# A hybrid-mixer and MoE layer kernel: the S5 rotation angles as one VectorE addition per pair instead of 16 GpSimd operations, and a second buffer for one held block

## The chip, the cores and the metric

One core of a Trainium2 chip runs the whole kernel in one launch. The time is device microseconds (us) of that core. Engines are called PE (TensorE), DVE (VectorE), ACT (ScalarE), POOL (GpSimd) and SP (SyncE, which issues most of the DMAs). Each runs its own instruction stream in order, and they meet only at semaphores.

## The reference, cut to what matters

The input is 512 tokens of width 2048. An input projection feeds four mixers of width 512 (S5, RG-LRU, RWKV7, SSD), an output projection follows, then a mixture of experts with 64 experts and two choices per token, and a final norm. The change touches the S5 mixer and the storing of the input projection:

```
dt = exp(log_dt);  mag = exp(lambda_re * dt)
abar = mag * (cos(lambda_im * dt) + i sin(lambda_im * dt))
state[t] = abar * state[t-1] + Bbar u[t]          # complex, 32 groups of 64 states
y = Re(C state) + d * u;  y = gelu(y);  y = y * sigmoid(y @ w_glu + b_glu);  rms_norm
```

The kernel takes the rotation out of the recurrence: it multiplies the input by exp(-i t theta), runs two real scans with the factor mag, and multiplies back by exp(i t theta). So it needs, for each of 128 states (two groups, a "pair"), the cosine and sine of t theta at all 512 times t. There are 16 pairs. The angle, in turns, is the sum of a fine part (t mod 32: 32 values) and a coarse part (t div 32: 16 values), both kept in `turns[:, p, 0:48]`.

## The kernel before, in words

**Projection.** PE first computes six ordinary column tiles (n = 0 to 5; loop at L2621 and L2627), four of which are the S5 input U5. Tile n may start once ACT has copied out tile n-2 (`proj_out`, L1118). All other columns are done as 16 "fast slabs" f of 256 columns by Strassen's method in Winograd's form: 7 products b = 0 to 6 of 8 K-slices each (L2660), where each K-slice is recorded as two matmuls of 256 columns. Product number g = 7f + b may start when ACT has taken product g-2 out of PSUM (`take_product`, L1132). Products 0, 2 and 4 go into the held blocks `held[0..2]`; POOL later adds each to a block that ACT stored (`add_held`, L912). ACT may fill held block k again once POOL has added the one of the slab before (semaphore `added`).

**Weight sums.** Some products need sums of weight blocks. POOL issues three accumulating DMAs per slab: `sum1` (L890), `sum2` (L895) and `sum3` (L899), for slab f+1 during slab f, at b = 3, 5 and 6. A fourth sum, needed by product (f, 3), is one 128x1024 addition: on DVE for f = 0 to 5 (`weight_sum`, L1662), on POOL from then on (L905). SP loads the weight blocks; the block for product g is asked for when product g-7 is done.

**S5 pairs.** PE places S5 work at fixed K-slices of the projection, counted by u, with u = 76 + 8g + k from the first fast slab on. One step comes every 25 K-slices: at step p (even) PE computes the inputs of pairs p and p+1 (`s5_in_mm`, L2461; it waits until DVE has read those of pair p-1), and at steps 5, 9, 13, 17 the outputs of four finished pairs (`s5_out_mm`, L2473). DVE runs `s5_pair(p)` in order (L1537, L1677, L1683, L1684, L1696, L1698), with the weight sums of slabs 0 to 5 at fixed half pairs: before pair 3, in the middle of pairs 5 and 7, before pairs 10 and 12, in the middle of pair 14.

**Angles and tables.** POOL's `wrap(p)` makes the 128x512 angles of a pair by 16 operations of 128x32 (L860), each adding one coarse value to the 32 fine ones. It writes into the second half of the pair's table buffer; there are three such buffers, so wrap(p) waits until pair p-3 is done with its tables. wrap(0 to 2) run ahead of the first sum1, wrap(3) and wrap(4) between sum1(0), sum2(0) and sum3(0), and the others behind given products:

```
            wrap_at = {(S5_EVERY * p - 112) // 8: p for p in range(5, NPAIR)}
```

ACT's `table(p, r)` (L1150 to L1154) waits for the angles and makes the cosine (r = 0) and sine (r = 1) by three activations each. Tables 0, 1 and 2 stand behind the copy of tile 1, tables 3 and 4 behind those of tiles 3 and 4, the others behind given products.

**After the S5 pairs** DVE makes the RG-LRU convolution, the norms, the SSD and RWKV7 steps; PE goes on through the slabs, the RWKV7 chunks, the output projection and the experts, whose weights stream from HBM.

Of the kernel before, what the change touches and what calls it, by code (L numbers as in the profile page):

```python
# [7 lines left out]
P = 128  # L8
# [96 lines left out]
def build(nc, I, out):  # L105
    with ExitStack() as ctx:
# [133 lines left out]
        held = [wo_more[:, 0, 0:256], wo_more[:, 0, 256:512], wo_more[:, 1, 0:256]]  # L240
# [244 lines left out]
        wrap_ok, WRAP = tr_used_act, 4  # L485
# [33 lines left out]
        def slabs_done(eng, n):  # L519
            eng.wait_ge(took, TOOK + PB_ * n)  # L520
            eng.wait_ge(added, ADDED + 3 * n)

# [275 lines left out]
        def _(pool):  # L798
# [56 lines left out]
            def wrap(p):  # L855
                turn = s5tab[p % 3][:, 1, :]
                if p >= 3:
                    pool.wait_ge(tab_used, p - 2)
                for k in range(COARSE):
                    last = nc.gpsimd.tensor_scalar(turn[:, FINE * k:FINE * k + FINE], turns[:, p, 0:FINE],  # L860
                                                   turns[:, p, FINE + k:FINE + k + 1], None, ALU.add)
                last.then_inc(wrap_ok, 1)

# [11 lines left out]
            for p in range(3):  # L875
                wrap(p)
# [30 lines left out]
            def add_held(f, k):  # L907

                n, t, reads = ((0, 1, 4), (1, 1, 5), (0, 0, 6))[k]
                pool.wait_ge(took, TOOK + PB_ * f + reads)  # L910
                o = block_out(f, n, t)
                nc.gpsimd.tensor_tensor(o, o, held[(1, 2, 0)[k]], ALU.add).then_inc(added, 1)  # L912

            sum1(0)
            wrap(3)
            sum2(0)
            wrap(4)
            sum3(0)
            wrap_at = {(S5_EVERY * p - 112) // 8: p for p in range(5, NPAIR)}
            for f in range(NF):  # L920
                for b in range(PB_):
                    if b == 0 and f >= S5_SUMS:
                        sum4(f)
                    if b == 3 and f < NF - 1:
                        sum1(f + 1)
                    if b == 4:
                        add_held(f, 0)
                    if b == 5:
                        add_held(f, 1)
                        if f == Z_END:  # L930
                            pool.wait_ge(dtv_ok, 2)
                            k, i = at[("xt", NTT - 1)]
                            pool.wait_ge(full[k], i + 1)
                            triangle(0)
                            triangle(1)
                        if f < NF - 1:
                            sum2(f + 1)
                    if b == 6:
                        add_held(f, 2)
                        if f < NF - 1:  # L940
                            sum3(f + 1)
                        if f in (Z_END + 1, Z_END + 2):
                            triangle(f - Z_END + 1)
                    if PB_ * f + b in wrap_at:
                        wrap(wrap_at[PB_ * f + b])

# [124 lines left out]
        def _(act):  # L1071
# [48 lines left out]
            def take_product(f, b):  # L1120

                act.wait_ge(prod_ok, PROD + PB_ * f + b + 1)
                if b in (0, 2, 4):
                    if f:

                        act.wait_ge(added, ADDED + 3 * f - (0, 2, 1)[b // 2])
                    to = held[b // 2]
# [18 lines left out]
            def table(p, r):  # L1146
                x, out = s5tab[p % 3][:, 1, :], s5tab[p % 3][:, r, :]
                if r == 0:
                    act.wait_ge(wrap_ok, WRAP + p + 1)
# [97 lines left out]
            for n in range(NT):  # L1247
                if n:
                    proj_out(n)
                if n == 1:  # L1250
                    s5_setup()
                    for p in range(3):
                        table(p, 0)
                        table(p, 1)
                if n in (3, 4):
# [228 lines left out]
        def _(dve):  # L1484
# [161 lines left out]
            v.do(nc.vector.tensor_reduce(out=stacked[:], in_=ident[:].rearrange("p (g t) -> p t g", g=2), op=ADD, axis=AX))  # L1646
            op(T4, B22, T1, ADD)
# [16 lines left out]
            def s5_pair(p):  # L1664
# [32 lines left out]
                v.settle()  # L1697
                v.tell(nc.vector.tensor_tensor(xi, k[0], k[2], ADD), st_ok, p + 1)  # L1698
# [1412 lines left out]
```

## Time and profile before

| | us |
|---|---|
| median of 3 runs | 2458.86 (2458.52 to 2463.66) |
| the profiled execution's own time | 2459.19 |
| its span, first to last instruction | 2457.4 |
| busy: PE / DVE / ACT / POOL | 2265.4 / 816.2 / 456.7 / 549.0 |
| mean granted TensorE clock | 0.971 |
| time outside the span | 1.8 |

The last line is the difference of the second and the third. Busy times of different engines lie beside each other and don't add up; a wait counts only where the chain that ended last runs through it. In the rows below a line number names the instruction's line of the kernel before, and "[x <- R]" is idle time of that engine just before the instruction, with what ended it.

### The profile page before, as it was taken

Reading aid. Unit: us, or ns where it says so; the run is one execution under the profiler, and the core shown is the slowest. Engines: PE = TensorE matmul, PEld = TensorE weight load, DVE = VectorE, ACT = ScalarE, POOL = GpSimd, SP = SyncE. Lnnn points to the kernel's source line nnn. Section 1 sums busy time; section 2 is a strip of 40 time slices with the busy share of each in tenths; the row PEclk is TensorE's granted clock in tenths of the full one; section 3 lists DMA queues with packets and bytes.
Section 4 is the critical chain, followed back from the end, with each engine's and each line's share of the span. In section 5 each row is a group of like instructions: output and inputs, shape, how many; then the busy total and the mean of one; then the engine's idle time right before and its main releaser. Section 6 shows DMA issues by size and latency. Waiting matters only on the chain.

```text
span 2457.4 us, 34178 instructions
## 1 busy us (share of the span) xinstructions
PE 2265.4 (92%) x13339; PEld 1302.2 (53%) x13339; DVE 816.2 (33%) x1331; ACT 456.7 (19%) x796; POOL 549.0 (22%) x845
## 2 busy tenths in 40 slices
PE   8999999999999999999998888888888898888888
PEld 4476868885566646544444444444444444444443
DVE  6689775256444332311111111111111111111114
ACT  3433262114222222000000000000000000000002
POOL 5799423331322110111111111111111111111110
PEclk9999999999999999999999999999999999999999
DMA  5477869873302445899999999999999999999998
GB/s 179 95 162 153 182 137 191 184 160 115 104 20 78 148 175 204 344 423 426 427 424 426 427 425 426 427 427 425 427 427 425 427 427 425 426 427 426 424 427 368
DMA packets 236939, 759.80 MB, mean 309 GB/s; under 512 B 35928, under 2 KB 173468, under 8 KB 193084
## 3 DMA queue, kind: packets, MB, share of 16 engines
q1 hardware_dynamic: 173464, 710.29, 72.3%
q0 software_dynamic: 54016, 42.00, 9.6%
q10 hardware_dynamic: 9380, 6.40, 0.8%
q8 instruction: 56, 0.92, 0.2%
q14 instruction: 23, 0.19, 0.0%
HBM read 753.23 MB, written 47.19 MB: 326 GB/s over the span
## 4 chain that ended last, share of the span: by engine, by line
PE 48%; DMA 41%; POOL 6%; DVE 3%; issue 1%; ACT 1%; SPq 0%; DVEq 0%; POOLq 0%; ACTq 0%
DMA big<-in_moe_w 39%; PE ps L3005 12%; PE ps L2660 12%; PE ps L2727 6%; POOL big L860 5%; PE ps L3036 4%; PE ps L2882 2%; PE ps L2802 1%; DMA big<-in_norm_final 1%; PE ps L3021 1%; PE ps L2627 1%; PE ps L2787 1%; PE ps L2989 1%; PE ps L2675 1%; PE ps L2495 1%
## 5 line engine op out<-in xcount | busy, mean ns | idle before, releaser
L3005 PE MATMUL ps<-big 128*64 128x384 f32 x4096 | 695.6, 494 | 96.4 <-DMA big<-in_moe_w 85.7
L3005 PEld LDWEIGHTS ps<-big 128*64 128x64 f32 x4096 | 305.3, 138 | 492.9 <-issue 343.6
L3036 PE MATMUL ps<-big 128*64 128x512 f32 x1536 | 386.7, 657 | 57.0 <-DVE big L2352 57.0
L2660 PE MATMUL ps<-big 128*128 128x256 f32 x1792 | 396.8, 382 | 8.1 <-ACT wo_more L1132 5.5
L2660 PEld LDWEIGHTS ps<-big 128*128 128x128 f32 x1792 | 340.3, 191 | 67.5 <-issue 14.5
L3036 PEld LDWEIGHTS ps<-big 128*64 128x64 f32 x1536 | 124.8, 150 | 272.0 <-issue 240.9
L2348 DVE TENSOR_SCALAR big<-ps,scal 128x384 f32<-128x384 f32 x64 | 39.6, 618 | 688.9 <-PE ps L3005 688.9
L2357 DVE SCALAR_TENSOR_TENSOR big<-ps,scal,big 128x512 f32<-128x512 f32 x128 | 90.2, 747 | 399.3 <-PE ps L3036 399.3
L1033 POOL COPY scal<-slots 128x3 f32 (+1 forms) x64 | 12.0, 188 | 909.7 <-DVE big L2357 891.4
L1454 ACT ACTIVATE big<-ps,scal 128x384 f32<-128x384 f32 x64 | 37.2, 581 | 799.4 <-PE ps L3005 770.8
L860 POOL TENSOR_SCALAR big<-big 128x32 f32<-128x32 f32 x256 | 160.1, 1449 | 0.1
L2727 PE MATMUL ps<-big 128*128 128x512 f32 x320 | 154.4, 611 | 1.0 <-ACT big L1217 0.7
L3021 PE MATMUL ps<-stacked,big 128*128 128x64 f32 x768 | 141.2, 334 | 0.0
L3021 PEld LDWEIGHTS ps<-stacked,big 128*128 128x128 f32 x768 | 138.8, 261 | 0.8 <-issue 0.8
L1459 ACT ACTIVATE big<-ps 128x192 f32<-128x192 f32 x64 | 21.2, 332 | 516.4 <-PE ps L3021 516.4
L1537 DVE TENSOR_TENSOR big<-big 128x512 f32<-128x512 f32 (+5 forms) x132 | 103.9, 807 | 20.8 <-ACT big L1173 10.1
L2727 PEld LDWEIGHTS ps<-big 128*128 128x128 f32 x320 | 55.9, 189 | 56.6 <-issue 50.8
L2272 DVE TENSOR_TENSOR big<-ps,gffn 128x512 f32<-128x512 f32 x128 | 82.5, 686 | 0.6
L2989 PEld LDWEIGHTS ps<-ident,big 128*128 128x128 f32 x512 | 62.0, 194 | 37.7 <-issue 37.7
L1029 POOL DMA_INDIRECT big<-x_rows,gix x62 | 65.2, 1052 | 54.4 <-POOL gix L1025 54.4
L912 POOL TENSOR_TENSOR big<-big,wo_more 128x256 f32<-128x256 f32 x48 | 56.5, 1239 | 84.3 <-ACT big L1132 57.6
L1043 POOL DMA_INDIRECT y_rows<-big,six x62 | 62.8, 1014 | 55.1 <-POOL six L1040 51.5
(444 smaller groups left out, 2003.4 us busy)
## 6 DMA issues: line engine op xcount, KB each, us to landing
big<-in_moe_w SPq DMA_DIRECT2D x187, 3072.0 KB, 38.7
big<-in_w_in SPq DMA_DIRECT2D x96, 512.0 KB, 4.4
big<-in_w_in POOLq DMA_DIRECT2D x32, 512.0 KB, 7.5
big<-in_moe_w SPq DMA_DIRECT2D x6, 1536.0 KB, 8.8
big<-big POOLq DMA_DIRECT2D x16, 512.0 KB, 5.3
big<-in_w_out SPq DMA_DIRECT2D x8, 1024.0 KB, 5.3
big<-y_rows SPq DMA_DIRECT2D x8, 1024.0 KB, 28.1
big<-in_x SPq DMA_DIRECT2D x4, 1024.0 KB, 8.4
```

Source lines behind the costliest of these rows:

```text
L860: last = nc.gpsimd.tensor_scalar(turn[:, FINE * k:FINE * k + FINE], turns[:, p, 0:FINE], turns[:, p, FINE + k:FINE + k + 1], None, ALU.add)
L1029: nc.gpsimd.indirect_dma_start(xg[k], None, x2g, bass.IndirectOffsetOnAxis(ap=of, axis=0), bounds_check=T * GR - 1, oob_is_err=False).then ...
L1043: nc.gpsimd.indirect_dma_start(ydg, bass.IndirectOffsetOnAxis(ap=six[k][:, 0:1], axis=0), yb[k], None, bounds_check=2 * T * GR - 1, oob_is ...
L1537: v.do(nc.vector.tensor_tensor(out, a, b, o))
L2272: nc.vector.tensor_tensor(xT[k][:, cs, :].rearrange("p c (g t) -> p c g t", g=GR), ps[h][:, 0:NJ * P // 2].rearrange("p (c g t) -> p c g t ...
L2357: nc.vector.scalar_tensor_tensor(out=yb[k][:, cs], in0=ps[5 + q][:], scalar=scal[k][:, 0:1], in1=yb[k][:, cs], op0=MUL, op1=ADD).then_inc( ...
L2660: last = nc.tensor.matmul(o, w[:, k, :], side[:, k, :], start=(k == 0 and b in (0, 1, 5)), stop=(k == 7), skip_group_check=True)
L2727: last = nc.tensor.matmul(ps[b][:], ready[c][:, P * i:P * i + P], wo_mix[c], start=(c == 0), stop=(c == PO - 1), skip_group_check=True)
L2989: last = nc.tensor.transpose(ps[h][:, P * j:P * j + P], xg[k].rearrange("t (p c) -> t c p", c=NJ)[:, c], ident[:])
L3005: last = nc.tensor.matmul(ps[2 + w][B * g:B * g + B, 0:FF], xT[k][:, j, B * g:B * g + B], W13[k][w][:, NJ * g + j, :], start=(j == 0), sto ...
L3021: last = nc.tensor.matmul(o, uv[k][:, w, :].rearrange("p (t c) -> p c t", c=FC)[:, m], stacked[:], start=True, stop=True)
L3036: last = nc.tensor.matmul(ps[5 + q][B * g:B * g + B, :], hid[k][:, m, :], W2[k][:, m, 512 * n:512 * n + 512], start=(m == 0), stop=(m == F ...
```

## The change

POOL's `wrap` and all its calls go. DVE makes the angles of a pair by one addition of 128x512 with both operands broadcast: those of pairs 0, 1 and 2 in its set-up, behind the reduction that makes `stacked` and ahead of the two 128x2048 operations of T4; those of pair p+3 inside `s5_pair(p)`, between the last product with the table and the last addition of the pair. ACT makes tables 0 and 1 behind the copy of tile 1 and table n behind the copy of tile n for n = 2, 3, 4. `held` gets a fourth block, which stands in for block 0 in slabs 1, 3, 5 and 7; in slabs below 8, ACT's wait before it fills block 0 asks for the additions of one slab less.

```
-        held = [wo_more[:, 0, 0:256], wo_more[:, 0, 256:512], wo_more[:, 1, 0:256]]
+        held = [wo_more[:, 0, 0:256], wo_more[:, 0, 256:512], wo_more[:, 1, 0:256], wo_more[:, 1, 256:512]]
...
+        HELD2 = 8
+        def held_of(f, k):
+            return held[3 if k == 0 and f % 2 and f < HELD2 else k]
...
-            def wrap(p):
-                turn = s5tab[p % 3][:, 1, :]
-                if p >= 3:
-                    pool.wait_ge(tab_used, p - 2)
-                for k in range(COARSE):
-                    last = nc.gpsimd.tensor_scalar(turn[:, FINE * k:FINE * k + FINE], turns[:, p, 0:FINE],
-                                                   turns[:, p, FINE + k:FINE + k + 1], None, ALU.add)
-                last.then_inc(wrap_ok, 1)
...
-            for p in range(3):
-                wrap(p)
...
-                nc.gpsimd.tensor_tensor(o, o, held[(1, 2, 0)[k]], ALU.add).then_inc(added, 1)
+                nc.gpsimd.tensor_tensor(o, o, held_of(f, (1, 2, 0)[k]), ALU.add).then_inc(added, 1)
             sum1(0)
-            wrap(3)
             sum2(0)
-            wrap(4)
             sum3(0)
-            wrap_at = {(S5_EVERY * p - 112) // 8: p for p in range(5, NPAIR)}
...
-                    if PB_ * f + b in wrap_at:
-                        wrap(wrap_at[PB_ * f + b])
...
-                        act.wait_ge(added, ADDED + 3 * f - (0, 2, 1)[b // 2])
-                    to = held[b // 2]
+                        act.wait_ge(added, ADDED + 3 * f - (0, 2, 1)[b // 2] - (3 if b == 0 and f < HELD2 else 0))
+                    to = held_of(f, b // 2)
...
-                    act.wait_ge(wrap_ok, WRAP + p + 1)
+                    act.wait_ge(angle_ok, ANGLE + p + 1)
...
-                    for p in range(3):
-                        table(p, 0)
-                        table(p, 1)
-                if n in (3, 4):
+                    table(0, 0)
+                    table(0, 1)
+                if 1 <= n <= 4:
                     table(n, 0)
                     table(n, 1)
...
+            def angles(p):
+                v.tell(nc.vector.tensor_tensor(s5tab[p % 3][:, 1, :].rearrange("p (a b) -> p a b", a=COARSE),
+                                               turns[:, p, FINE:].unsqueeze(2).to_broadcast([P, COARSE, FINE]),
+                                               turns[:, p, 0:FINE].unsqueeze(1).to_broadcast([P, COARSE, FINE]), ADD), angle_ok, ANGLE + p + 1)
+            for p in range(3):
+                angles(p)
             op(T4, B22, T1, ADD)
...
                 v.tell(nc.vector.tensor_tensor(k[2], cosT, k[3], MUL), tab_used, p + 1)
                 v.settle()
+                if p + 3 < NPAIR:
+                    angles(p + 3)
+                    v.settle()
                 v.tell(nc.vector.tensor_tensor(xi, k[0], k[2], ADD), st_ok, p + 1)
```

## Rows read from the trace of the kernel before

**Rows 1.** The chain that ended last, by engine and by line, whole run.

```profile
PE 48%; DMA 41%; POOL 6%; DVE 3%; issue 1%; ACT 1%; SPq 0%; DVEq 0%; POOLq 0%; ACTq 0%
DMA big<-in_moe_w 39%; PE ps L3005 12%; PE ps L2660 12%; PE ps L2727 6%; POOL big L860 5%; PE ps L3036 4%; PE ps L2882 2%; PE ps L2802 1%; DMA big<-in_norm_final 1%; PE ps L3021 1%; PE ps L2627 1%; PE ps L2787 1%; PE ps L2989 1%; PE ps L2675 1%; PE ps L2495 1%
```

**Rows 2.** Windows: stretch, length, busy us (count) per engine, granted clock, DMA share, GB/s.

```profile
84.00:88.00 4.00, 3.01 (x8) 1.14 (x10) 3.91 (x5) 1.31 (x3) 0.00 (x0) 0.60 1.10 298
236.00:240.00 4.00, 3.27 (x8) 2.64 (x9) 3.93 (x6) 3.60 (x7) 4.00 (x6) 0.50 0.49 58
300.00:500.00 200.00, 200.00 (x917) 163.64 (x916) 106.39 (x152) 70.27 (x107) 68.11 (x53) 1.00 0.84 175
1600.00:2400.00 800.00, 700.68 (x3788) 342.72 (x3787) 127.34 (x211) 68.31 (x106) 88.41 (x173) 0.96 1.01 426
```

**Rows 3.** The chain that ended last, 0 to 800 us: start, us, what.

```profile
55.45 24.39 POOL big L860 x48
```

**Rows 4.** Timeline of PE, 50 to 300 us: start, us, work, [idle before <- releaser].

```profile
84.99 8.69 PE L2621 MATMUL ps<-big 128*64 128x512 f32 x32 [2.53 <-ACT big L1118]
...
146.68 1.53 PE L2660 MATMUL ps<-big 128*128 128x256 f32 x6 [1.75 <-DMA big<-big]
...
176.06 9.73 PE L2660 MATMUL ps<-big 128*128 128x256 f32 x44 [0.74 <-DMA big<-big]
...
212.84 11.06 PE L2660 MATMUL ps<-big 128*128 128x256 f32 x50 [1.30 <-ACT wo_more L1132]
...
236.74 7.09 PE L2660 MATMUL ps<-big 128*128 128x256 f32 x20 [4.25 <-ACT wo_more L1132]
...
258.52 32.99 PE L2660 MATMUL ps<-big 128*128 128x256 f32 x150
291.44 1.92 PE L2473 MATMUL ps<-big 128*32 128x512 f32 x16
```

**Rows 5.** Timeline of ACT, same columns, 50 to 330 us.

```profile
79.87 0.72 ACT L1150 ACTIVATE big<-big,zero 128x512 f32<-128x512 f32 x1 [4.75 <-POOL big L860]
...
236.30 0.38 ACT L1132 ACTIVATE wo_more<-ps 128x256 f32<-128x256 f32 x1 [11.39 <-POOL big L912]
```

**Rows 6.** Timeline of POOL, same columns, 50 to 320 us.

```profile
235.21 0.99 POOL L912 TENSOR_TENSOR big<-big,wo_more 128x256 f32<-128x256 f32 x1
```

**Rows 7.** POOL by line, 55 to 262 us: work, count, busy us, mean ns, idle before.

```profile
L860 POOL TENSOR_SCALAR big<-big 128x32 f32<-128x32 f32 x256 | 160.1, 1449 | 0.1
```

**Rows 8.** Timeline of DVE, 38 to 320 us: steps of S5 pairs 0, 1 and 3.

```profile
77.58 2.75 DVE L1537 TENSOR_TENSOR big<-big 128x512 f32<-128x512 f32 x4
80.25 0.68 DVE L1696 TENSOR_TENSOR big<-big 128x512 f32<-128x512 f32 x1
80.96 0.69 DVE L1698 TENSOR_TENSOR big<-big 128x512 f32<-128x512 f32 x1
...
88.01 2.75 DVE L1537 TENSOR_TENSOR big<-big 128x512 f32<-128x512 f32 x4
...
126.33 1.75 DVE L1696 TENSOR_TENSOR big<-big 128x512 f32<-128x512 f32 x1
```

**Rows 9.** Timeline of DVE: weight sum 0 and every later idle up to weight sum 5.

```profile
116.26 1.23 DVE L1662 TENSOR_TENSOR big<-big 128x1024 f32<-128x1024 f32 x1 [5.88 <-DMA big<-in_w_in]
...
146.73 1.22 DVE L1662 TENSOR_TENSOR big<-big 128x1024 f32<-128x1024 f32 x1 [0.66 <-DMA big<-big]
...
176.11 1.26 DVE L1662 TENSOR_TENSOR big<-big 128x1024 f32<-128x1024 f32 x1 [6.19 <-DMA big<-big]
...
233.43 1.25 DVE L1662 TENSOR_TENSOR big<-big 128x1024 f32<-128x1024 f32 x1 [3.98 <-DMA big<-big]
...
258.63 1.89 DVE L1537 TENSOR_TENSOR big<-ps,big 128x512 f32<-128x512 f32 x3 [1.73 <-PE ps L2461]
...
268.01 1.23 DVE L1662 TENSOR_TENSOR big<-big 128x1024 f32<-128x1024 f32 x1 [2.16 <-PE ps L2660]
```

**Rows 10.** DVE by line and shape, 39 to 45.7 us: additions and products with broadcast operands.

```profile
L1537 DVE TENSOR_TENSOR big<-tk,s5v 128x768 f32<-128x768 f32 x2 | 1.8, 954 | 0.0
```

More of the change, by code:

```diff
@@ L482, in build @@
         WEIGHT_IN = [16 * len(PA), 16 * (len(PB) + 2), 16 * 8, 0, 16 * ((len(slabs) + 1) // 2), 16 * (len(slabs) // 2), NTT]
-        wrap_ok, WRAP = tr_used_act, 4
+        angle_ok, ANGLE = tr_used_act, 4
         s1_in, s2_in, s3_in = xg_in[0], xg_in[1], y_out[0]
```

## The prediction

> **What bounds the kernel now.** I began with the page's chain of work that ended last: PE holds 48% of it and DMA 41%, almost all of that the expert weights, and one POOL line, L860, holds 5% [rows 1]. L860 is what the change removes, so 5% of 2457.4 us (123 us) looks like the prize. It is not, for a chain names one engine for each stretch and doesn't say how close the next one runs behind. The windows answer that: in the expert stage the DMA share is 1.01 at 426 GB/s, and from 300 to 500 us PE is busy for 200.00 of 200 us at full clock [rows 2]. Neither stretch can gain; both can only start earlier. The chain's pieces with L860 begin at 55 us [rows 3] and end near 236 us, and there the question is how much PE, which runs in a fixed order from the first tile to the experts, really stood still.
>
> So I went to PE's timeline. From 50 to 292 us it has five idle stretches: 2.53 + 1.75 + 0.74 + 1.30 + 4.25 = 10.57 us [rows 4]. Behind the first and the last the granted clock lay low, 0.60 from 84 to 88 us and 0.50 from 236 to 240 us, the lower level (1.2 GHz) for part or all of these windows [rows 2]. The first costs (1 - 0.60) x 4 = 1.6 us. For the last I count: 20 matmuls took 7.09 us, at the pace of the later row (32.99 us for 150, or 0.220 us each) they take 4.40, so 2.7 us more [rows 4]. Together PE lost 10.57 + 1.6 + 2.7 = **14.9 us**.
>
> Who held PE each time? At 82.5 us it waited for ACT's copy of tile 2, which stood behind table 2, and ACT waited 4.75 us for L860 [rows 4, 5]: POOL needed 24.39 us for three pairs [rows 3]. At 146.7 and 176.1 us it waited for a DMA within SBUF (sum2), which POOL issues in order behind its wraps [rows 4]. At 212.8 us it was ACT again. At 236.7 us PE waited for ACT, which had waited 11.39 us for POOL's addition of a held block, itself only done at 235.21 + 0.99 us [rows 4 to 6]. Here 16 operations, a sum2 and its DMA wait stood ahead of the addition. POOL had no time to spare: L860 took 160.1 us of the 207 from 55 to 262 us, and before it POOL was idle for 0.1 us [rows 7].
>
> **The change part by part.**
>
> *Wraps off POOL.* The 256 operations keep POOL busy for 160.1 us, 0.63 us each (the mean of 1.449 us counts records that overlap) [rows 7]. Off the path they are worth nothing; on it they are worth PE's four stalls from 146 us on, and the first by way of ACT. What POOL has left are three DMA issues and three additions per slab. Is a transfer late next? From 300 to 500 us no wraps are there, the slabs follow each other as densely, and PE has no idle time [rows 2]. So I take nothing for the DMAs. If that cover is gone, a late sum costs what it does now, 0.7 to 1.8 us each [rows 4].
>
> *Order of the tables on ACT.* Table 2 moves behind the copy of tile 2. ACT makes tables 0 and 1 by about 75 us, as now (its wait for table 2 began at 79.87 - 4.75 = 75.1) [rows 5], copies tile 2, and tile 4 starts on PE at 82.5 us. The 2.53 us go, and with them I expect the low clock to go; if that comes from tile 4 itself, 1.6 us stay. Tables 3 and 4 need angles that DVE makes at the end of pairs 0 and 1, about 81 and 93 us, in time for copies at 83 and 90 us within 3 us that nobody waits for.
>
> *Second held block.* ACT's wait of 11.39 us has two answers in this change, the wraps' removal and this buffer. Either would do, so it gets no gain of its own. If POOL were still late, it would be worth up to the 4.25 + 2.7 us [rows 4].
>
> *Angles on DVE.* The trace has no 128x512 sum of two broadcast SBUF operands. The nearest row has the same forms at 768 elements: 0.954 us [rows 10]. A 128x512 of two plain SBUF operands takes 0.68 us, and starts of two that wait for each other lie 80.96 - 80.25 = 0.71 us apart [rows 8]. Bounds: 0.954 x 512/768 = 0.64 us from below, and from above 1.75 us, which the instruction of 0.68 us took when it met POOL's addition [rows 8]. I take **0.71 us**, from the rows of the same size. The three of the set-up, 2.1 us, lie in DVE's idle 10 us before pair 0 and delay only T4, needed at product 6. Ten of the other 13 (pairs 3 to 12) are in the stretch that matters.
>
> *What is late next: DVE.* Its tightest meeting with PE is weight sum 5, in pair 14. DVE's real work from weight sum 0 (start 116.26) to the end of sum 5 (268.01 + 1.23 = 269.24) is 152.98 us less the idle 0.66 + 6.19 + 3.98 + 1.73 + 2.16 = 14.72, so 138.26 us [rows 9]. Sum 0 waits for a weight block asked for at the end of tile 5, so it moves with PE: 116.26 - 2.53 - 1.6 = 112.1. With ten angles DVE is through sum 5 at 112.1 + 138.3 + 7.1 = 257.5 if it never idles. The DMA waits in this list are all of the kind that earlier sums shorten, so it hardly will. POOL's additions slow DVE where they meet (1.75 against 0.68) [rows 8], and a tenth of its old time (14.72 of 152.98) was idle, in which some of them fell; I add 0.8 us: **258.3 us**.
>
> PE needs it at product (5, 3), which is 60 matmuls into the row that starts at 258.52: 258.52 + 60 x 0.220 = 271.7 [rows 4]. Without the 14.9 us that is **256.8 us**. PE thus waits 1.5 us for DVE. The two earlier meetings (inputs of pairs 12 and 14) come out within half a microsecond. Pair 15 ends some 16 us behind sum 5 (half of pair 14 and pair 15 at 10.5 us each, and collisions), 274.5, and PE wants it at 291.44 - 14.9 + 1.5 = 278.0, so nothing more is lost.
>
> *Sum.* 14.9 - 1.5 = 13.4 us. From 292 us on every start hangs on PE's order or on buffers that it frees, so the expert stream starts as much earlier and the gain passes whole. 2459.19 - 13.4 = 2445.8 for the profiled execution. That execution lies 0.3 us over the median of the runs, so I say **2445.5 us**.
>
> *A rule to weigh.* DVE's four products of a pair took 2.75 us both while POOL ran 48 wraps (at 77.58) and while POOL had nothing to do (at 88.01) [rows 8], so by the rows taking wraps away gives DVE nothing. The Trainium skill, page "SBUF — State Buffer", section "SBUF: two separate sides", says otherwise: a DVE operation with two SBUF inputs and a GpSimd operation that reads SBUF take turns on one port pair, and whoever comes second is blocked for the whole instruction. By that, DVE would get time back here and the 1.5 us of waiting would go: 2444. On POOL's side the trace may bear it out (0.63 us per wrap over all, but 24.39/48 = 0.51 in the first three pairs, where DVE was idle for 10 us) [rows 3, 7], and DVE's 1.75 us beside an addition of POOL as well [rows 8]. By the same rule each new addition can hold up a POOL addition for 0.7 us, which POOL now has room for.
>
> **Rivals.**
>
> *A. PE alone is the bound.* DVE keeps up, because collisions are fewer or POOL's two-input additions fall into PSUM reads. Gain 14.9 us: 2444.0, and if the restarts behind the five stalls cost a little more than I counted, 2442.5. For it: the margin is only 1.5 us, and the page's rule. Against: DVE would have no idle left at all.
>
> *B. DVE becomes the real bound.* Each addition costs more like 1.2 us, or the collisions double as POOL and DVE now meet in every slab. Ten times 0.4 us more: gain 9 us, 2450. For it: the row of 1.75 us. Against: most steps of a pair show 0.68 to 0.71.
>
> *C. The stalls move to the weight DMAs.* PE now asks for blocks some 8% faster, sum2 waits for its block and PE for sum2. Four waits of 1.5 us and one low clock of 2.7 us take 9 us back: gain 4 to 5 us, 2455. Against: the dense stretch from 300 us [rows 2].
>
> *D. Slower.* DVE is in order, and the addition stands ahead of the state that PE waits for. If it costs c instead of 0.71 us, the gain 13.4 falls by 10(c - 0.71); it is gone at c = 2.05 us and the kernel is 5 us slower at c = 2.55 us, 2464. That takes a collision in every pair, each longer than the longest shown; this mechanism decides nothing below 2 us.
>
> *E. It doesn't do what it says:* the first stall stays, since tile 4 waits for something else too. Gain 13.4 - 4.1, 2449.5; counted with B.
>
> **How the numbers follow.** Forecast (2445.5, its own range 2443.5 to 2447.5): 50%. A 20%, B and E 19%, C 8%, D 3%. 0.2% is 4.9 us, about what a measurement of this kernel tells from no change. Faster by more: the forecast, A, B and half of C, 0.93. Within: half of C and a third of D, 0.05. Slower: 0.02. The range runs from 2441.5 (A with its margin) to 2450.5 (B), and leaves out C and D, 11%, and some at the low end.
>
> **What would show it.** PE without idle at 82 us and at 232 us, and no low clock behind them. POOL's busy time lower by 150 us or more and DVE's higher by 16 x 0.6 to 0.7 us, about 11. sum2(1) and sum2(2) issued some 10 us earlier against PE's product. If the forecast is right, DVE has next to no idle from pair 3 to pair 15, PE has one or two waits for DVE (L1662 or L1677) of 2 us together between 190 and 260 us, and output step 17 starts near 278 us (277 under A, 282 under B). An angle addition over 1 us would make the step on DVE wrong; PE waiting for DMA within the slabs would make C right; an expert stream that doesn't start 13 us earlier would make the passing on wrong.

## The result and the profile after

The changed kernel took **2439.62 us** (median of 4 runs, 2438.55 to 2445.99), the kernel before beside it 2461.26 (4 runs); ratio 0.9916, 95% interval 0.9892 to 0.9940. The forecast was 2445.5 us, in a range of 2441.5 to 2450.5. The kernel is faster, as said, but by the ratio the gain is 0.0084 x 2461.26 = 20.7 us, half as large again as the 13.4 of the sum, and the time lies 1.9 us under the range. The profiled execution took 2440.12 us with a span of 2438.4; before it was 2459.19 and 2457.4, so 19.0 us of span.

The page's chain of work that ended last, by engine and by line, beside [rows 1]:

```profile
PE 52%; DMA 44%; DVE 2%; issue 1%; ACT 0%; POOL 0%; ACTq 0%; DVEq 0%; SPq 0%; POOLq 0%
DMA big<-in_moe_w 43%; PE ps L2657 16%; PE ps L3002 10%; PE ps L2724 6%; PE ps L2624 3%; PE ps L3033 3%; PE ps L2879 2%; PE ps L2799 1%; DMA big<-in_norm_final 1%; PE ps L2784 1%; PE ps L3018 1%; PE ps L2458 1%; PE ps L2672 1%; PE ps L2492 1%; PE ps L2900 1%
```

POOL's 6% are 0% and no POOL line is left. PE and DMA have taken the share over, which is the point of the first section of the prediction: the 5% of L860 were not the prize.

Three of the windows of [rows 2] (stretch, length, busy us of PE, PEld, DVE, ACT and POOL, granted clock, DMA share, GB/s):

```profile
84.00:88.00 4.00, 4.00 (x22) 1.41 (x20) 3.93 (x6) 3.10 (x5) 0.00 (x0) 1.00 1.11 301
236.00:240.00 4.00, 4.00 (x21) 3.51 (x20) 3.93 (x5) 2.82 (x5) 1.82 (x3) 1.00 0.73 178
...
1600.00:2400.00 800.00, 699.82 (x3802) 343.09 (x3798) 127.72 (x211) 68.19 (x105) 85.85 (x168) 0.97 1.01 426
```

The clock stands at 1.00 where it was 0.60 and 0.50. The stretch of the experts is what it was, DMA share 1.01 at 426 GB/s. It only begins earlier: PE's first expert product starts at 976.02 us where it started at 994.93.

PE's timeline from 50 to 300 us (start, us, work); beside [rows 4]:

```profile
82.25 7.09 PE L2618 MATMUL ps<-big 128*64 128x512 f32 x32
...
143.72 21.85 PE L2657 MATMUL ps<-big 128*128 128x256 f32 x100
165.51 1.99 PE L2458 MATMUL ps<-big 32*128 32x512 f32 x8
...
242.62 32.64 PE L2657 MATMUL ps<-big 128*128 128x256 f32 x150
275.19 1.92 PE L2470 MATMUL ps<-big 128*32 128x512 f32 x16
```

No row of this view shows idle time any more. Tile 4 takes 7.09 us instead of 8.69, and output step 17 starts at 275.19 instead of 291.44: **16.25 us** at the end of the S5 stage. Product (5, 3), which the prediction took for the tightest meeting with DVE, starts 60 matmuls into the row of 242.62, 242.62 + 60 x 32.64/150 = 255.7 us. The row at 165.51 is the input step of pairs 8 and 9.

DVE's timeline, beside [rows 8, 9]; L1635 is the addition of the angles, L1656 the weight sum, and L1671 the instruction with which DVE is through reading a pair's inputs:

```profile
56.11 1.88 DVE L1635 TENSOR_TENSOR big<-big 128x512 f32<-128x512 f32 x3
...
80.77 0.69 DVE L1635 TENSOR_TENSOR big<-big 128x512 f32<-128x512 f32 x1
...
111.90 1.23 DVE L1656 TENSOR_TENSOR big<-big 128x1024 f32<-128x1024 f32 x1 [5.18 <-DMA big<-in_w_in]
...
163.04 0.68 DVE L1671 TENSOR_TENSOR big<-ps,big 128x512 f32<-128x512 f32 x1
...
180.28 3.16 DVE L1524 TENSOR_TENSOR big<-big 128x512 f32<-128x512 f32 x4
...
251.87 1.22 DVE L1656 TENSOR_TENSOR big<-big 128x1024 f32<-128x1024 f32 x1
```

The three additions of the set-up start at 56.11 and lie in idle time. Within a pair one takes 0.69 us, and its neighbours start 0.72 us apart, as priced. From the start of sum 0 (111.90) to the end of sum 5 (251.87 + 1.22 = 253.09) DVE works 141.2 us without idle time; the sum in the prediction had 146.2 and an end at 258.3. The row at 180.28 is a hold-up, a DVE operation that takes longer than usual beside a POOL addition: 3.16 us where 2.75 is usual. The longest single one in this stretch is 0.54 us. DVE is 2.6 us early for product (5, 3) (253.1 against 255.7), but less for the inputs: it has read those of pair 7 at 163.04 + 0.68 = 163.7 and PE comes for them at 165.5, 1.8 us later, and at the step of pairs 12 and 13 2.0 us later (212.9 against 214.95).

POOL's timeline, beside [rows 6, 7]:

```profile
122.09 1.09 POOL L907 TENSOR_TENSOR big<-big,wo_more 128x256 f32<-128x256 f32 x1
125.22 0.73 POOL L907 TENSOR_TENSOR big<-big,wo_more 128x256 f32<-128x256 f32 x1 [2.03 <-ACT wo_more L1120]
...
173.10 1.53 POOL L885 DMA_DIRECT2D big<-in_w_in  x1 [13.81 <-DMA big<-in_w_in]
```

POOL waits for DMAs and for ACT, and each held-block addition runs alone, soon after ACT's store. Busy time of POOL fell from 549.0 to 400.6 us, that of DVE rose from 816.2 to 820.9 where 16 additions alone are 11 us, so everything else on DVE takes some 6 us less. The prediction's signs were 150 us or more and about 11 us; POOL's fall of 148.4 is just under the one, DVE's rise of 4.7 far under the other.

### The profile page after: what moved, and what is told of

Read it like the earlier page. It is cut to its first block, busy times and chain, and to the rows that moved or that the text cites. A ratio compares the mean times of both kernels' runs of the same rounds, so it can differ in the third digit from the quotient of the medians.

```text
span 2438.4 us, 33939 instructions
## 1 busy us (share of the span) xinstructions
PE 2248.5 (92%) x13339; PEld 1294.0 (53%) x13339; DVE 820.9 (34%) x1347; ACT 456.3 (19%) x796; POOL 400.6 (16%) x589
## 4 chain that ended last, share of the span: by engine, by line
PE 52%; DMA 44%; DVE 2%; issue 1%; ACT 0%; POOL 0%; ACTq 0%; DVEq 0%; SPq 0%; POOLq 0%
DMA big<-in_moe_w 43%; PE ps L2657 16%; PE ps L3002 10%; PE ps L2724 6%; PE ps L2624 3%; PE ps L3033 3%; PE ps L2879 2%; PE ps L2799 1%; DMA big<-in_norm_final 1%; PE ps L2784 1%; PE ps L3018 1%; PE ps L2458 1%; PE ps L2672 1%; PE ps L2492 1%; PE ps L2900 1%
## 5 line engine op out<-in xcount | busy, mean ns | idle before, releaser
L3018 PE MATMUL ps<-stacked,big 128*128 128x64 f32 x768 | 141.2, 334 | 0.0
L2986 PE MATMUL ps<-ident,big 128*128 128x128 f32 x512 | 74.1, 288 | 1.6 <-DMA big<-x_rows,idxg 1.6
L1444 ACT ACTIVATE big<-big,scal 128x1024 f32<-128x1024 f32 x64 | 72.8, 1137 | 0.0
```

The lines of the kernel that those rows point to most:

```text
L1444: nc.scalar.activation(yb[k], xg[k], ACT.Copy, scale=scal[k][:, 2:3]).then_inc(pre_ok[k], 1)
L2986: last = nc.tensor.transpose(ps[h][:, P * j:P * j + P], xg[k].rearrange("t (p c) -> t c p", c=NJ)[:, c], ident[:])
L3018: last = nc.tensor.matmul(o, uv[k][:, w, :].rearrange("p (t c) -> p c t", c=FC)[:, m], stacked[:], start=True, stop=True)
```

## The experiments

"Step 17" is the start of PE's last S5 output. It was 291.44 us in the trace before and 275.19 in the one after. The line numbers of each row are those of that run's own kernel.

**Which part of the change does it?** Four kernels, each with one part undone or one done alone.

e1, the changed kernel with the old order of tables:

```
+                    for p in range(3):
+                        table(p, 0)
+                        table(p, 1)
+                if n in (3, 4):
...
-                if 1 <= n <= 4:
```

> The changed kernel, but ACT makes tables 0, 1 and 2 behind the copy of tile 1, as before. Theory 1 (the angles' early arrival is all that counts): DVE has the angles of pair 2 by 58 us, ACT is through table 2 at about 79.5 us and copies tile 2 at 80.1, before PE wants it at 82.3 us. PE has no idle time at tile 4, output step 17 starts at 275.2 us as in the changed kernel, total within 1 us of it. Theory 2 (the new order carries the first stall, as the prediction had it): PE stops at 82 us, the clock falls behind it, step 17 starts 3 to 4 us later, 278.5 to 279.

Step 17 at 275.20 us, no idle time on PE; 2443.43 us (4 runs, 2439.98 to 2446.05), ratio 0.9920 (0.9898 to 0.9941). ACT's timeline (L1142 ends table 2, L1107 copies tiles 2 and 3):

```profile
78.51 0.72 ACT L1142 ACTIVATE big<-big,minus_halfpi 128x512 f32<-128x512 f32 x1
79.26 0.60 ACT L1107 ACTIVATE big<-ps 128x512 f32<-128x512 f32 x1
```

With angles from DVE table 2 ends at 79.23 and the copy is made at 79.26, three microseconds before PE needs it at 82.3. Theory 1 holds for the stage: once DVE makes the angles, the new order is worth nothing there.

e2, the changed kernel with one held block 0 (`HELD2 = 0`, and ACT's wait as before):

> The changed kernel with the held block 0 single again. Theory 1 (either answer would do): with the wraps gone POOL adds the held block within 1 to 2 us of ACT's store, ACT never waits for it, PE has no idle time, step 17 at 275.2 us, total within 1 us of the changed kernel. Theory 2 (the buffer carries part of the gain): ACT waits for POOL at some product 0 of slabs 1 to 7 and PE stops, step 17 later than 276 us.

Step 17 at 275.22 us, no idle time on PE, no wait of ACT for POOL; 2444.40 us (4 runs, 2440.28 to 2446.23), ratio 0.9926 (0.9903 to 0.9949). Theory 1 again: the second buffer does nothing once POOL is on time. Both theories also said a total within 1 us of the changed kernel; the two medians lie 3.8 and 4.8 us over its first one (2439.62), but 0.4 and 1.3 us over its second one (2443.06, e10 below). What differs lies behind step 17. The kernel without both parts at once was not run.

e3, the kernel before with the second held block alone:

```
-                to = held[b // 2]
+                to = held_of(f, b // 2)
```

> The kernel before with the second held block alone; wraps stay on POOL. Theory 1 (the stall at 232 us comes from the held block): ACT's wait of 11.4 us goes, and of PE's 4.25 us idle and 2.7 us of low clock about 5.5 us go, since sum2 of slab 4 lands only about 233.4 us and holds PE for under 1 us: step 17 at 285 to 286.5 us. Theory 2 (POOL is late by itself, whoever waits for it first): PE stops at product 2 or 3 of slab 4 or at a table instead, and the gain is under 2 us, step 17 at 289.5 us or later.

2459.19 us (10 runs), ratio 0.9993 (0.9981 to 1.0005), step 17 at 294.12: nothing gained (the kernel before had step 17 at 291.44 to 294.30, see e7 and e12). Three of PE's rows with idle time, and POOL's wrap 4 (L866), its sum2 (L901) and the wrap behind it:

```profile
84.13 7.09 PE L2627 MATMUL ps<-big 128*64 128x512 f32 x32 [1.76 <-ACT big L1124]
...
114.03 9.29 PE L2666 MATMUL ps<-big 128*128 128x256 f32 x34 [3.36 <-ACT big L1124]
...
239.53 7.25 PE L2666 MATMUL ps<-big 128*128 128x256 f32 x20 [4.16 <-DMA big<-big]
```

```profile
97.24 11.86 POOL L866 TENSOR_SCALAR big<-big 128x32 f32<-128x32 f32 x16
...
231.86 0.90 POOL L901 DMA_DIRECT2D big<-big  x1 [5.60 <-DMA big<-in_w_in]
232.49 5.49 POOL L866 TENSOR_SCALAR big<-big 128x32 f32<-128x32 f32 x16
```

ACT's 11.4 us wait went, and PE stopped just as long at 239.5 for sum2. POOL had issued that one late because it first had to see sum1 land, and sum1 stood behind two wraps (issued at 221.44, against 201.47 in the changed kernel). Theory 2: POOL is late, whoever waits first. A new stall stands at 114.03: wrap 4 took 11.86 us where it had taken 8.33, so table 4 and with it the copy of tile 5 came late. Here the first stall was shorter and tile 4 took 7.09 us, so PE ran 2.5 us ahead of the trace before, and this too was given back at 114.03.

e6, the kernel before with the angles of pairs 0 to 2 on DVE and the new order of tables:

```
-            for p in range(3):
-                wrap(p)
```

> The kernel before with the angles of pairs 0, 1 and 2 on DVE and the new order of the tables; wraps 3 to 15 stay on POOL, one held block. Theory 1 (stalls add up): the first stall and its low clock go (4.1 to 4.3 us), the later ones stay as they are, step 17 at 287.2 us. Theory 2 (POOL sets the pace from 115 to 236 us): PE is 4.3 us earlier at 105 us and waits longer later; at step 17 under 2 us are left, 289.5 us or later.

2461.29 us (10 runs), ratio 0.9993 (0.9981 to 1.0006), step 17 at 294.64. Two of PE's rows with idle time:

```profile
114.05 10.60 PE L2664 MATMUL ps<-big 128*128 128x256 f32 x34 [5.08 <-ACT big L1116]
...
239.85 6.14 PE L2664 MATMUL ps<-big 128*128 128x256 f32 x20 [4.01 <-ACT wo_more L1130]
```

The first stall is gone and 5.08 us stand at 114 us in its place: wrap 4 took 11.49 us here, for PE and with it DVE's pair 2 came earlier (95.09 us instead of 99.25) and fell onto the wrap. Theory 2, and more than it said: with this part alone the 4 us are given back within 32 us. So the stalls don't add up. POOL sets the pace from about 90 to 236 us, and of the kernels run only those that relieve POOL over that whole stretch gain. Moving wraps 3 to 15 alone was not tried.

**Why was DVE not late?**

e4, each addition of pairs 3 to 15 made twice:

```
+                    op(s5tab[p % 3][:, 1, :]..., turns[:, p + 3, FINE:]..., turns[:, p + 3, 0:FINE]..., ADD)
+                    v.settle()
                     angles(p + 3)
```

> The changed kernel with the addition of the angles of pairs 3 to 15 made twice in a row, same place. In the changed kernel weight sum 5 ends at 253.1 us and PE starts product (5, 3) at 255.7, so DVE has 2.6 us of room. Theory 1 (DVE was not the bound, but only just): ten more additions of 0.72 us put sum 5 at 260.3, PE waits for DVE by 4.6 us in all, step 17 starts at 279.5 to 280.2 us. Theory 2 (DVE has far more room than this, its order gives way): step 17 stays within 1 us of 275.2. Theory 3 (more two-input operations on DVE also meet POOL more, as the prediction's 0.8 us supposed): sum 5 later than 262 us, step 17 later than 281.5.

2446.78 us (4 runs), ratio 0.9945 (0.9930 to 0.9960). PE's rows with idle time:

```profile
166.44 1.99 PE L2462 MATMUL ps<-big 32*128 32x512 f32 x8 [0.80 <-DVE big L1671]
...
203.24 14.48 PE L2661 MATMUL ps<-big 128*128 128x256 f32 x66 [1.53 <-DVE big L1656]
218.75 1.99 PE L2462 MATMUL ps<-big 32*128 32x512 f32 x8 [1.02 <-DVE big L1671]
...
260.52 20.09 PE L2661 MATMUL ps<-big 128*128 128x256 f32 x92 [1.32 <-DVE big L1656]
```

PE waits for DVE four times, 4.67 us in all: for the inputs of pairs 8 and 12 and for weight sums 3 and 5. The prediction had named sum 5 and the inputs of pair 12. Sum 5 ends at 260.37, and step 17 comes at 280.54, 5.35 us late. Theory 1's mechanism, a shade above its band. DVE's room is real and small: ten times 0.72 us use it up and cost PE the rest. The first of the four waits comes at the meeting with 1.8 us of room.

e5, small POOL operations in POOL's idle time:

```
+                        if f < 6:
+                            for k in range(COARSE):
+                                g.do(nc.gpsimd.tensor_scalar(spare[:, FINE * k:FINE * k + FINE], spare_in[:], spare_in[:, k:k + 1], None, ALU.add))
+                            g.settle()
```

> The changed kernel, and POOL also runs 16 additions of 128x32 like a wrap (values that nobody reads, in buffers of their own) behind sum3 of slabs 1 to 6, where it is idle for some 13 us while DVE works on the pairs. DVE's work from the start of sum 0 to the end of sum 5 is 141.2 us without them. Theory A (small POOL operations don't slow DVE; what made DVE faster in the changed kernel is that POOL's 128x256 additions no longer come in bunches): it stays at 141 to 142, and 16 of them take POOL 11 to 12.5 us each time. Theory B (each takes the port from DVE): 5 x 16 of them cost DVE 4 us or more, 145 us and up, and PE waits for it. Under A step 17 stays at 275.2 to 276 us, under B it comes at 277 or later.

2444.12 us (4 runs), step 17 at 275.36. DVE's sums 0 and 5, and two of POOL's groups of 16:

```profile
111.54 1.22 DVE L1662 TENSOR_TENSOR big<-big 128x1024 f32<-128x1024 f32 x1 [4.64 <-DMA big<-in_w_in]
...
251.91 1.23 DVE L1662 TENSOR_TENSOR big<-big 128x1024 f32<-128x1024 f32 x1
```

```profile
213.46 12.93 POOL L938 TENSOR_SCALAR big<-spare_in 128x32 f32<-128x32 f32 x16
...
242.68 11.19 POOL L938 TENSOR_SCALAR big<-spare_in 128x32 f32<-128x32 f32 x16
```

From 111.54 to 251.91 + 1.23 are 141.6 us, against 141.2 without 80 extra operations (141.2 to 141.3 in all six traces of such kernels). Theory A: they don't slow DVE by more than 0.4 us in all. DVE slows them: 11.2 to 12.9 us for 16, where the three first wraps of the kernel before, with DVE idle for 10 of 24 us, took 8.1 each [rows 3].

e9, the same 18 held-block additions, but in slabs 0 to 5 in a row:

```
-                    if b == 4:
-                        add_held(f, 0)
...
                     if b == 6:
+                        if f < 6:
+                            add_held(f, 0)
+                            add_held(f, 1)
                         add_held(f, 2)
```

> The changed kernel, but in slabs 0 to 5 POOL does the three held-block additions back to back behind the last product of the slab instead of each behind its own. Nothing else is added, the same 18 additions. In the changed kernel DVE needs 141.2 us from the start of sum 0 to the end of sum 5, and its longest single hold-up beside an addition of POOL is 0.54 us; in the kernel before single hold-ups reached 1.77 us where two additions stood in a row. Theory 1 (bunches cost DVE more than the same additions apart): 143 to 146 us, hold-ups of over 1 us, and if sum 5 ends after 255.7 us PE waits for it. Theory 2 (each addition costs the same wherever it stands): 140.5 to 142 us, no hold-up over 0.6 us. The output step 17 of PE at 275.2 us under theory 2, up to 277 under theory 1.

Step 17 at 276.65; one run, 2441.14 us. Two of POOL's bunches, then DVE's operations beside them, and sum 5:

```profile
128.42 4.33 POOL L907 TENSOR_TENSOR big<-big,wo_more 128x256 f32<-128x256 f32 x3
...
208.86 1.73 POOL L907 TENSOR_TENSOR big<-big,wo_more 128x256 f32<-128x256 f32 x2
```

```profile
131.13 3.62 DVE L1528 TENSOR_TENSOR big<-big 128x512 f32<-128x512 f32 x4
...
206.62 4.52 DVE L1528 TENSOR_TENSOR big<-big 128x512 f32<-128x512 f32 x4
...
254.89 1.22 DVE L1660 TENSOR_TENSOR big<-big 128x1024 f32<-128x1024 f32 x1
```

DVE's work from sum 0 (112.13) to the end of sum 5 (256.11) is 144.0 us, 2.8 more than with the additions apart, and PE waits 1.29 us for it at the input step of pair 12. Four operations of 2.75 us take 3.62 beside the first bunch and 4.52 beside the other, there with a single hold-up of 1.77 us. That is theory 1. It bears out bunches as a cause, and 2.8 us of the difference.

The rest can be read off the traces. For every instruction of DVE between sum 0 and sum 5 I took what it needed beyond the usual time of its kind in the trace after, and added these up. POOL makes 15 held-block additions in this stretch in each of the four traces.

| trace | hold-ups, us in all | of these beside a POOL addition | longest |
|---|---|---|---|
| before | 8.9 | 8.4 | 1.77 |
| after | 4.5 | 4.5 | 0.54 |
| e9, bunched | 7.3 | 7.3 | 1.77 |
| e5, with 80 small operations | 5.0 | 4.6 | 0.55 |

The longest one before, beside three additions of POOL in 4.4 us (at 193.73 and 195.71); two of these DVE operations take 1.29 us elsewhere:

```profile
194.52 3.06 DVE L1537 TENSOR_TENSOR big<-big 128x512 f32<-128x512 f32 x2
```

So the same 15 additions cost DVE 8.4 us before and 4.5 after. Beside wraps alone it loses 0.6 us, in more than a hundred instructions.

**How firm are the times themselves?**

e7 and e12, the kernel before again:

> The kernel before once more, for how much one execution differs from another. Theory 1 (the S5 stage of the kernel before is a chain by way of POOL whose wraps take 5.5 to 12.4 us each, depending on what DVE does beside them): step 17 is not at 291.44 to the tenth but somewhere from 290 to 295 us. Theory 2 (only the clock at the routing stage varies, 30.5 or 34.6 to 36.6 us from the first triangle product to the first down product): step 17 at 291.4 within 0.3 us. Both can hold for the routing stage.

> The kernel before a third time. Its step 17 stood at 291.44 us in the trace that the prediction used and at 293.85 in the second. Theory 1 (the S5 stage of the kernel before differs from one execution to the next, since it hangs on how POOL's wraps fall against DVE's operations): again another time, between 290 and 295 us, and PE's stalls from 140 to 275 us again of other lengths. Theory 2 (two fixed patterns): 291.4 or 293.9 within 0.2 us with the same stalls.

2460.89 and 2458.73 us, step 17 at 293.85 and 294.30. PE's rows with idle time behind 120 us, e7 and then e12:

```profile
148.63 1.60 PE L2661 MATMUL ps<-big 128*128 128x256 f32 x6 [3.66 <-DMA big<-big]
...
239.12 6.05 PE L2661 MATMUL ps<-big 128*128 128x256 f32 x20 [3.94 <-ACT wo_more L1133]
...
270.37 23.55 PE L2661 MATMUL ps<-big 128*128 128x256 f32 x108 [1.18 <-DMA big<-big]
```

```profile
148.68 1.90 PE L2662 MATMUL ps<-big 128*128 128x256 f32 x6 [3.84 <-DMA big<-big]
...
239.02 5.97 PE L2662 MATMUL ps<-big 128*128 128x256 f32 x20 [3.56 <-ACT wo_more L1134]
...
270.82 23.55 PE L2662 MATMUL ps<-big 128*128 128x256 f32 x108 [1.81 <-DMA big<-big]
```

The stall of [rows 4] at 146.7 us lasts twice as long here, those at 176.1 and 212.8 us are missing, a new one stands at 270. With 291.44 this makes three times out of one program, and two of them share a pattern: theory 1 for the spread, with something of theory 2's patterns in it. In all six traces of kernels with the angles on DVE, POOL's additions where they belong and one addition per pair (after, e1, e2, e8, e10, e11) step 17 lies between 275.19 and 275.22.

At the routing stage the kernel chooses each token's experts. It runs from the first product with a triangular matrix ("triangle product") to the first expert's second product ("down product"), and fillers are matmuls whose results nobody reads, which keep PE busy in between.

e10, the changed kernel again, and e8 and e11, the changed kernel with more fillers:

```
-            keep_busy(24)
+            keep_busy(32)
...
-            keep_busy(8)
+            keep_busy(14)
...
-            keep_busy(4)
+            keep_busy(10)
```

> The changed kernel with more filler matmuls at the routing stage: 32, 14 and 10 in place of 24, 8 and 4, so that PE's idle times there (2.0, 1.6 and 1.6 us) are mostly filled. In five traces so far this stage took 30.5 us without a low clock and 34.6 to 36.6 with one, in the same program. Theory 1 (the clock falls after PE's idle times): no low clock there, 30.5 to 31.5 us, median time 2438 to 2439.5, spread under 4 us. Theory 2 (the clock falls whatever PE does there, by what runs elsewhere): the stage takes 35 us in some runs as before, and the median stays at 2440 to 2444.

> The changed kernel once more, beside the one with more fillers. Theory 1 (the low clock at the routing stage comes in some executions and not in others, and each costs 4 to 6 us there): times between 2438 and 2447, median 2441 to 2443.5; the S5 stage as before, step 17 at 275.2 us. Theory 2 (the first measurement's median of 2439.6 is the typical one): median 2439 to 2440.5.

> The kernel with 32, 14 and 10 fillers once more, beside the changed kernel on the same chip. Theory 1 (fillers keep the clock up): 2439.4 to 2442.3 as the first time, median 2440 to 2441, 1 to 3 us under the changed kernel's of the same call, routing stage 30.5 us. Theory 2 (the first five runs were lucky): the same median as the changed kernel's, with runs over 2444.

e10: 2443.06 us (6 runs, 2437.99 to 2445.90), ratio 0.9928 (0.9914 to 0.9942). e8: 2440.52 (5 runs), ratio 0.9915 (0.9901 to 0.9928). e11: 2440.01 (5 runs), ratio 0.9917 (0.9903 to 0.9932). PE's timeline and a window of 4 us at the routing stage, of e10 and then of e8:

```profile
960.38 0.39 PE L2928 MATMUL ps<-big,tris 128*128 128x8 f32 x2 [2.03 <-DVE big L2193]
...
966.33 2.45 PE L2949 MATMUL ps<-big,ones 128*128 128x256 f32 x8
```

```profile
964.00:968.00 4.00, 4.00 (x34) 3.63 (x34) 0.55 (x3) 0.00 (x0) 1.01 (x1) 0.50 0.06 23
```

```profile
963.77 0.39 PE L2927 MATMUL ps<-big,tris 128*128 128x8 f32 x2 [0.25 <-DVE big L2192]
...
967.76 1.31 PE L2948 MATMUL ps<-big,ones 128*128 128x256 f32 x8
```

```profile
968.00:972.00 4.00, 4.00 (x36) 3.97 (x34) 2.65 (x9) 0.00 (x0) 2.16 (x2) 1.00 0.15 43
```

In e10 the clock falls to 0.50 behind PE's idle 2.03 us and the products behind it take nearly twice as long (2.45 us for 8 where e8 has 1.31). The stage from the first triangle product to the first down product takes 35.2 us in e10, 34.6 in the trace before, 36.6, 34.8, 36.2 and 36.4 in e1, e2, e6 and e5, and 30.5 in the trace after, e3, e4, e7, e9 and e12. The idle time ahead of it was 2.03 or 2.04 us in all of these. With the idle times filled it took 30.5 in both traces.

But the stage ends where the clock falls next. The first two down products of e8, right behind it:

```profile
994.27 7.07 PE L3033 MATMUL ps<-big 128*64 128x512 f32 x24 [0.81 <-DVE big L2349]
...
1015.59 5.37 PE L3033 MATMUL ps<-big 128*64 128x512 f32 x24 [0.81 <-DVE big L2349]
```

The first one takes 7.07 us instead of 5.37, with a granted clock of 0.84 from 992 to 996 us and 0.73 from 996 to 1000. It is so in e11 (7.07), in the trace after (7.00), in e4, e9 and e12, and in e10 in spite of its low clock before. The two traces with fillers thus have the low clock where the trace after, without them, has it: the fillers did not do away with it. And there is a fall with PE busy throughout: 0.50 from 576 to 580 us in the trace after, 0.50 from 592 to 596 in the one before, none in e10, where PE reaches the routing stage 3.35 us earlier (960.38 against 963.73). What makes the clock fall in one execution and not in another stays open.

The ten filler runs lie within 2437.08 to 2442.62 (median 2440.3), the ten of the changed kernel within 2437.99 to 2445.99 (median 2441.4). e8's median of 2440.52 misses theory 1's 2438 to 2439.5 and lies in theory 2's band, and e11's 2440.01 is 3.1 us under the changed kernel's beside it. So the spread speaks for theory 1. The clock right behind the stage speaks for theory 2, and for the median the two kernels' intervals overlap. That the fillers are worth anything is not shown.

## Why the prediction was wrong

**What the miss is made of.** For the profiled execution the sum said 2445.8 us, and 2440.12 was measured, 5.7 us less. Of these, 1.5 us are a wait for DVE that did not come, 1.35 us lie in stalls counted too small, and 2.8 us lie behind step 17, where the prediction had no term at all. The first is the step whose mechanism failed, the last is the largest.

**Where the gain is.** Right: five stalls of PE on chains that all go back to POOL, their removal, the clock behind two of them, and a gain that the later stages pass on. From step 17 to the end are 2166.0 us before and 2163.2 after. e1 and e2, the same up to step 17, have 2169.1 and 2167.0: the passing on is whole, give or take what the stages behind it do.

**The size of the stalls.** 14.9 us were counted, 16.25 came. Behind each of the four later stops PE also needed some 0.1 to 0.3 us more to get going than the idle time says (143.7 to 165.5 us shows 100 matmuls in 21.8 us; between 200.5 and 223.8 before, the same work and 1.30 us of idle took 23.3), together 0.8 us. 0.35 us went in the row of 258.52, which took 32.99 us for what now takes 32.64, and by 0.15 us PE was earlier already at 71 us. Rival A had 1.5 us for restarts; they are 0.8 of the 1.35.

**DVE the next bound: the step that failed.** "DVE is through sum 5 at 258.3 us", "PE thus waits 1.5 us". It was through at 253.1 and PE did not wait. The price of the addition was right (0.72 against 0.71), so was the start (111.90 against 112.1). The mis-sized term is the 138.3 us of "real work", taken over from the kernel before, with 0.8 us added for more collisions. It contained 8.9 us of DVE's hold-ups, nearly all beside POOL's additions, and these come close together because the wraps that the change removes make POOL late. 141.2 less ten angles at 0.72 are 134.0: 4.3 us less, not 0.8 more, and the hold-ups fell by 4.4 (8.9 to 4.5). The prediction saw one of 1.07 us (1.75 instead of 0.68) [rows 8] and used it as a bound for a price instead of asking whether it would still be there. e9 brings 2.8 us back by bunching alone, and e5 clears the wraps themselves. So in mechanism rival A, which had 20%, was the case: PE alone is the bound. Its time of 2444.0 or 2442.5 was not. The room is 1.8 us at the inputs of pair 8, not at sum 5, which the prediction called the tightest meeting and which has 2.6; e4 shows where it ends.

**Time back for DVE.** The Trainium skill, page "SBUF — State Buffer", section "SBUF: two separate sides", says that a DVE operation with two SBUF inputs and a GpSimd operation that reads SBUF block each other for a whole instruction. By that DVE was to get time back, against the prediction's reading of its row, and it did. But the time came from the additions of 128x256, not from the wraps: wraps of 32 columns cost DVE nothing that e5 could show. The row itself was a weaker proof than it looked, for at 88.01 POOL was not without work, it issued a DMA at 88.56 and began wrap 3 at 89.76. On POOL's side the traces agree with that page of the Trainium skill: 16 wraps take 5.5 to 13 us, depending on what DVE does meanwhile. They differ from it in that the block is not mutual for these small operations.

**Two answers to one wait.** "Either would do" was wrong for the kernel before: the held block alone gained nothing (e3), since the next wait for POOL stood behind it. It was right only for the changed kernel, where it isn't needed. Likewise the first stall: the order of the tables does nothing there (e1), early angles do it all.

**The range, and what lies behind step 17.** Between the traces before and after, the routing stage went from 34.6 to 30.5 us and the first down product from some 5.4 to 7.0, together 2.5 of the 2.8 us. That is the clock falling at another place and not the change: in e10 the changed kernel took 35.2 us for the routing stage, and in e7 and e12 the kernel before took 30.5. It is luck of this pair of traces. Without it even the corrected sum, 2459.19 - 16.25 = 2442.9, lies inside the range: the two mis-sized terms alone would not have taken the time out of it, and the ten runs' median of 2441.4 lies at its edge. The prediction went from one execution (2459.19) and took it for typical within 0.3 us. Its step 17 at 291.44 was the earliest of three (293.85, 294.30), and 46 runs of the kernel before have their median at 2460.9 (2455.6 to 2467.4). For the changed kernel ten runs have theirs at 2441.4, so 19.5 us between the medians. Of these 16.3 to 19.1 lie ahead of step 17, by these three traces; the rest lies behind it, where the clock accounts for a part. Executions with the same 30.5 us for the routing stage still differ there (2162.7 us from step 17 to the end in e12, 2165.3 in e7), which was not taken apart. Three of the first four runs of the changed kernel came out at its quick end. The range had no term for any of this, though the clock's two levels stood in the trace.

## What to carry to other kernels

When an engine that is late by itself is relieved, ask for each work time that you carry over how much of it was collision with the bunches that the lateness made: they go with it. Relief of one waiter does nothing as long as the late engine sets the pace: parts of such a change measured alone (0.9993 and 0.9993) said nothing about the whole (0.992). And take two or three traces of the kernel before, since a stage that hangs on two engines' interleaving differs between executions by more than the effect of many an edit.

## What the runs showed of the hardware

Sixteen GpSimd additions of 128x32 took from 5.5 us (POOL at 232.5 us in e3, DVE idle throughout) to 12.9 us (e5 at 213.5, DVE busy), while DVE lost next to nothing to 80 of them: 141.6 against 141.2 us. A GpSimd addition of 128x256 with two inputs takes 0.72 us alone and holds a DVE operation up by 0.34 to 0.54 us once (trace after). The same 15 additions, most of them in rows of two and three, cost DVE 7.3 us instead of 4.5 (e9). And after about 2 us of PE idle the granted clock fell to the lower level in some executions of a kernel and not in others (34.6 to 36.6 us against 30.5 for the routing stage). With the idle times filled down to 0.25 us it stayed up in that stage in both traces, and fell in the first down product behind it (7.07 us against 5.37). It also fell with PE busy throughout (0.50 from 576 to 580 us in the trace after).
